# S5 states scanned in units of two pairs under the weight strips, with the unit's stores begun from ScalarE

## The reference

```
z = h @ w_in                                  # 1024 -> 5120 columns; u is 1024 of them
x_re = einsum('tbgc,gpc->tbgp', ug, bb_re)    # 64 groups of 16 channels, 64 complex states each
x_im = einsum('tbgc,gpc->tbgp', ug, bb_im)
h[t] = lam_bar * h[t-1] + x[t]                # diagonal, complex, the associative scan
y = einsum(h_re, c_re) - einsum(h_im, c_im) + d * u
y5 = gelu(y)
```

## Time and profile before

| quantity | value |
|---|---|
| median of 3 runs | 3718.71 us (3714.18 to 3720.71) |
| the profiled execution, its own time | 3713.49 us |
| its span, first to last instruction | 3711.7 us |
| PE busy | 3191.5 us, 86% |
| DVE busy | 1431.3 us, 39% |
| ACT busy | 1003.4 us, 27% |
| POOL busy | 936.7 us, 25% |
| TensorE clock granted, mean | 0.892 of full |
| DMA moved | 421.74 MB, 114 GB/s mean |

### The profile page before, as it was taken

One profiled execution on the slowest core, in us unless ns is written; L12 is line 12 of the kernel. 1 busy time (PEld: TensorE's weight loads), 2 busy tenths in 40 slices (PEclk: granted clock), 3 DMA queues, 4 the chain that ended last, 5 costly groups with the idle time before them and its releaser, 6 DMA issues. The chain is left out here.

```text
span 3711.7 us, 46938 instructions
## 1 busy us (share of the span) xinstructions
PE 3191.5 (86%) x16972; PEld 2891.6 (78%) x16972; DVE 1431.3 (39%) x2425; ACT 1003.4 (27%) x1675; POOL 936.7 (25%) x461
## 2 busy tenths in 40 slices
PE   7999985789938787499499978999999949999599
PEld 6999984678737676299488848999999948889487
DVE  6893396111961088443200022000000057776422
ACT  3211112211101143333200023111111168887122
POOL 2222340112501176011111200111111136554021
PEclk8999996999969999699799987999999966666799
DMA  4436332664325365442423222222222122323433
GB/s 129 127 122 206 117 98 61 167 179 137 108 70 157 113 239 162 165 119 85 170 90 110 82 79 88 68 68 68 68 77 76 51 100 89 113 85 99 158 136 109
DMA packets 374896, 421.74 MB, mean 114 GB/s; under 512 B 39937, under 2 KB 325249, under 8 KB 367665
## 3 DMA queue, kind: packets, MB, share of 16 engines
q1 hardware_dynamic: 204368, 315.69, 27.0%
q10 hardware_dynamic: 170464, 105.23, 9.1%
HBM read 273.66 MB, written 151.39 MB: 115 GB/s over the span
## 5 line engine op out<-in xcount | busy, mean ns | idle before, releaser
L1072 PE MATMUL p_psum<-p_h_hi,p_w_hi 128*128 128x344 f32 (+1 forms) x1600 | 566.4, 354 | 0.8 <-ACT p_y L777 0.8
L1072 PE MATMUL p_psum<-p_h_hi,p_w_lo 128*128 128x344 f32 (+1 forms) x1600 | 560.9, 351 | 0.0
L1072 PE MATMUL p_psum<-p_h_lo,p_w_hi 128*128 128x344 f32 (+1 forms) x1600 | 559.5, 350 | 0.0
L400 PE MATMUL p_psum<-p_h_hi,p_w_hi 128*128 128x408 f32 (+1 forms) x1280 | 448.5, 350 | 0.9 <-DVE p_h_lo L326 0.9
L400 PE MATMUL p_psum<-p_h_hi,p_w_lo 128*128 128x408 f32 (+1 forms) x1280 | 448.2, 350 | 0.0
L400 PE MATMUL p_psum<-p_h_lo,p_w_hi 128*128 128x408 f32 (+1 forms) x1280 | 448.0, 350 | 0.0
L1218 PE MATMUL c_psum<-c_wo_hi,c_m_hi 128*128 128x512 f32 (+1 forms) x816 | 319.2, 391 | 76.6 <-POOL c_m_lo L1202 76.6
L678 POOL CAST p_w_hi<-p_w_raw 128x1024 fp32r<-128x1024 f32 x80 | 105.5, 1319 | 936.5 <-PE p_psum L1072 772.8
L1072 PEld LDWEIGHTS p_psum<-p_h_hi,p_w_hi 128*128 128x128 f32 x1600 | 301.6, 189 | 34.0 <-issue 7.1
L1072 PEld LDWEIGHTS p_psum<-p_h_hi,p_w_lo 128*128 128x128 f32 x1600 | 301.6, 189 | 29.0
L1072 PEld LDWEIGHTS p_psum<-p_h_lo,p_w_hi 128*128 128x128 f32 x1600 | 301.7, 189 | 28.1
(11 more groups left out here) (276 smaller groups left out, 5599.8 us busy)
## 6 DMA issues: line engine op xcount, KB each, us to landing
p_w_raw<-in_w_in SPq DMA_DIRECT2D x112, 512.0 KB, 4.1
z<-p_out ACTq DMA_DIRECT2D x64, 512.0 KB, 3.2
z<-p_out ACTq DMA_DIRECT2D x32, 1024.0 KB, 5.6
hg_raw<-z SPq DMA_DIRECT2D x16, 2048.0 KB, 9.4
rt_raw<-z SPq DMA_DIRECT2D x16, 1536.0 KB, 7.0
p_u<-u_s SPq DMA_DIRECT2D x32, 584.0 KB, 7.9
c_m_raw<-m SPq DMA_DIRECT2D x16, 1024.0 KB, 6.7
u_s<-p_out SPq DMA_DIRECT2D x128, 73.0 KB, 3.3
```

What stands on the lines that cost most here:

```text
L400: ins = pe.matmul(psum[:, b, 0:n], w[par][:, k, :], h[:, k, c0:c0 + n], start=(k == 0 and j == 0), stop=(k == KD - 1 and j == 2))
L1072: ins = pe.matmul(bank, wv[par][:, k, :], h[:, k, c0:c0 + n], start=(k == 0 and j == 0), stop=(k == KD - 1 and j == 2))
```

## The change

The two jobs "into" and "out" and the scan over all pairs are replaced by one job, "unit", of two pairs (`UP = 2`, so `NU = 16` units a half), in strips 22 to 37 of the first half and 10 to 25 of the second. For each unit PE makes the contributions before the strip (`into`), DVE turns, scans and turns back the states of the two pairs while the strip runs (`unit`), and PE makes the outputs behind the strip (`out`). The scan is now the instruction `tensor_tensor_scan` with a real decay `mag8`; the complex turn is taken out by tables `turn_re` and `turn_im` of 32 x 129 elements each, which DVE makes once, ahead of the setup (`further`). The tile `x` is gone; the tables of the setup and the unit's tiles share one tile, `shared`. The loads of a unit (`load_unit`) are four: `wk`, `km`, `gs`, `u`. The gelu and the four stores of a unit are in ACT's list (`unit_stores`). Four loads fill `s_stack` at the start. The credit on `y_mm` is 2, and `y_mm` counts finished units.

```diff
-STRETCHES = (((0, 2, None), (2, 2, None), (4, 4, "setup"), (8, 12, "setup"), (20, 2, None), (22, 8, "into"),
-              (30, 8, None), (38, 2, None)),
-             ((0, 2, None), (2, 6, "out"), (8, 2, "out"), (10, 8, "into"), (18, 8, None), (26, 8, "out"),
-              (34, 4, None), (38, 2, None)))
+STRETCHES = (((0, 2, None), (2, 2, None), (4, 4, "setup"), (8, 12, "setup"), (20, 2, None), (22, 16, "unit"),
+              (38, 2, None)),
+             ((0, 2, None), (2, 6, None), (8, 2, None), (10, 16, "unit"), (26, 12, None), (38, 2, None)))
@@ SP
+            for c in range(2):
+                for q in range(2):
+                    sp.dma_start(s_stack[c * NP:(c + 1) * NP, :, q, :], a["s5_s0"][q * NP:(q + 1) * NP, c, :, :])\
+                        .then_inc(s5_ld, 16)
+            def load_unit(half, n, i, par):
+                sp.dma_start(wk[par], wt_dram[bass.ds(n * UP, UP)].rearrange("j p c n -> p j c n"))\
+                    .then_inc(slot_ld[par], 16)
...
-                            sp.wait_ge(x_mm, i * 8 + (32 * half + 4 * (q0 + par) + 4))
...
+                        if job == "unit":
+                            sp.wait_ge(y_mm, i * 2 + (NU * hf + par + 2))
+                            load_unit(hf, i * 2 + par, i, par)
...
+                    sp.wait_ge(k_done, NPAIR + 2)
+                    sp.wait_ge(kmat_st, 16 * L8)
@@ DVE, ahead of the setup's tables
+                dve.tensor_tensor(ta, turn_re[:, js, near], at_re, ALU.mult)
+                dve.tensor_tensor(tb, turn_im[:, js, near], at_im, ALU.mult)
+                dve.tensor_tensor(tc, turn_re[:, js, near], at_im, ALU.mult)
+                link(dve.tensor_tensor(td, turn_im[:, js, near], at_re, ALU.mult))
+                dve.tensor_tensor(turn_re[:, js, far], ta, tb, ALU.subtract)
+                link(dve.tensor_tensor(turn_im[:, js, far], tc, td, ALU.add))
+            k = 1
+            while k < CHH:
+                for part in range(max(1, k * NPAIR // D)):
+                    jn = min(NPAIR, D // k)
+                    further(k, part * jn, jn)
+                k *= 2
@@ DVE, a unit
+                step(dve.tensor_tensor(m_re[:, :, :, 1:XC], got[:, :, :, NS + 1:IN], re[:, :, :, 1:XC], ALU.mult))
+                step(dve.tensor_tensor(m_im[:, :, :, 1:XC], got[:, :, :, NS + 1:IN], im[:, :, :, 1:XC], ALU.mult))
...
+                        step(dve.tensor_tensor_scan(h_turned[:, jj, c, :], decay, h_in[:, jj, c, :], 0.0,
+                                                    ALU.mult, ALU.add))
@@ PE
-            pe.sem_inc(x_mm, 8)
-            pe.sem_inc(y_mm, 8)
+            pe.sem_inc(y_mm, 2)
...
+                pe.wait_ge(slot_ld[par], i * 64 + (64 * (NU // 2) * half + 64))
+                pe.wait_ge(hs_done, at + 1)
...
+                        if job == "unit":
+                            into(hf, i, par)
                         strip(hf, s0, i, par)
+                        if job == "unit":
+                            out(hf, i, par)
```

More of the change, by code:

```diff
@@ L545, in stores_before @@
             return CREDIT + sum(store_units(h, k) for h in range(2) for k in range(s % 2, N_P0, 2) if (h, k) < (hf, s))
[L547 to L554, removed]
         block = ctx.enter_context(nc.Block())
@@ L622, in two @@
                                     .then_inc(g_st[e], 16)
[L623 to L629, removed]
                 rounds(sp, n // 2, two)
@@ L653, in _ @@
             for s0, n, job in STRETCHES[1]:
[L654 to L658, removed]
+                if job == "unit":
                     for par in range(2):
                         sp.wait_ge(stored[par], stores_before(1, N_U + par))
-                if job == "out" and s0 > 20:
-                    sp.wait_ge(x_mm, 64 + 8)
                 strips(1, s0, n, job)
-            sp.wait_ge(scan_done, 3)
+            sp.wait_ge(hs_done, 2 * NU + 1)
             sp.dma_start(out_p, h_last[:]).then_inc(out_st, 16)
             sp.wait_ge(out_st, 32)
-            for pp in range(SLOT):
-                sp.wait_ge(y_st[pp], 32 * 2 * NSLOT + CREDIT)
+            for par in range(2):
+                sp.wait_ge(y_st[par], 64 * NU + CREDIT)
         @block.gpsimd
@@ L772, in two @@
[L772 to L778, removed]
@@ L779, in strips @@
-                rounds(act, n // 2, two)
+                        if job == "unit":
+                            act.wait_ge(y_mm, i * 2 + (NU * hf + par + 3))
+                            act.wait_ge(y_st[par], i * 64 + (64 * (NU // 2) * hf + CREDIT))
+                            for jj in range(UP):
+                                ins = act.activation(y[par][jj], ps[:, 6 + jj, 0:2 * YCH]
+                                                     .rearrange("p (q n) -> p q n", q=2), ACT.Gelu_apprx_tanh)
+                            ins.then_inc(y_done, 1)
+                            unit_stores(hf, i, par)
@@ new lines, in strips, with unit_stores @@
+                rounds(act, n // 2, two)
+            def unit_stores(half, i, par):
+                at = i * 2 + (NU * half + par)
+                act.wait_ge(y_done, at + 2)
+                for jj in range(UP):
+                    for c in range(2):
+                        row = (2 * UP * par + 2 * jj + c) * GC
+                        act.dma_start(y_dram[half, bass.ds(i * (4 * UP * GC) + row, GC), :, :]
+                                     .rearrange("o t c -> t o c"), y[par][jj][:, c, :]).then_inc(y_st[par], 16)
@@ L914, in _ @@
             dve.wait_ge(setup_done, 1)
+            dve.tensor_copy(cos8[:], cos[:])
+            dve.tensor_copy(sin8[:], sin[:])
+            link(dve.tensor_copy(mag8[:], mag[:]))
+            for _ in range(3):
+                dve.tensor_tensor(t0[:], cos8[:], cos8[:], ALU.mult)
+                dve.tensor_tensor(t1[:], sin8[:], sin8[:], ALU.mult)
+                dve.tensor_tensor(turns[:], cos8[:], sin8[:], ALU.mult)
+                link(dve.tensor_tensor(red[:], mag8[:], mag8[:], ALU.mult))
+                dve.tensor_tensor(cos8[:], t0[:], t1[:], ALU.subtract)
+                dve.tensor_scalar(sin8[:], turns[:], 2.0, None, ALU.mult)
+                link(dve.tensor_copy(mag8[:], red[:]))
@@ L916, in power_products @@
+            link(ins)
+            for c in range(2):
+                ins = dve.tensor_tensor(s_new[:, c], s_new[:, c], s_tmp[:, c], ALU.add)
+            ins.then_inc(setup_done, 1)
+            dve.wait_ge(setup_done, 2)
             def power_products(j, base, first, tmp, c):
@@ L1022, in stacks @@
-            def stacks(half):
-                with dve.Fori(0, NPAIR // 2) as i:
-                    for par in range(2):
-                        dve.wait_ge(y_mm, i * 2 + (NPAIR * half + par + 7))
-                        for q in range(2):
-                            for c in range(2):
-                                ins = dve.tensor_copy(h_stack[par][c * NP:(c + 1) * NP, q, :],
-                                                      x[q * NP:(q + 1) * NP, c, bass.ds(i * 2 + par, 1), NS:NS + YCH]
-                                                      .rearrange("p j n -> p (j n)"))
-                        ins.then_inc(hs_done, 1)
@@ new lines, in units @@
+            def units(half):
+                with dve.Fori(0, NU // 2) as i:
+                    for par in range(2):
+                        unit(half, i, par)
+            for e in range(2):
+                dve.wait_ge(wt_st[e], 16 * (NPAIR // 2) + CREDIT)
+                dve.wait_ge(g_st[e], 16 * (NPAIR // 2) + CREDIT)
+            dve.wait_ge(k_done, NPAIR + 2)
+            link(dve.memset(h_in[:, :, :, 0], 0.0))
+            dve.sem_inc(step_done, 1)
+            dve.sem_inc(hs_done, 1)
@@ L1074, in strip, with into, out @@
                     ins.then_inc(blk_done, 1)
+            def into(half, i, par):
+                at = i * 2 + (NU * half + par)
+                pe.wait_ge(slot_ld[par], i * 64 + (64 * (NU // 2) * half + 64))
+                pe.wait_ge(hs_done, at + 1)
+                for jj in range(UP):
+                    for q in range(2):
+                        for c in range(2):
+                            ins = pe.matmul(ps[q * NP:(q + 1) * NP, 4 + jj, c * IN:(c + 1) * IN],
+                                            wk[par][:, jj, c, q * NP:(q + 1) * NP],
+                                            u[par][:, 2 * jj + q, 0:IN], start=True, stop=True)
+                ins.then_inc(x_mm, 1)
+            def out(half, i, par):
+                at = i * 2 + (NU * half + par)
+                pe.wait_ge(hs_done, at + 2)
+                pe.wait_ge(y_done, at + 1)
+                for jj in range(UP):
+                    for q in range(2):
+                        bank = ps[:, 6 + jj, q * YCH:(q + 1) * YCH]
+                        pe.matmul(bank, km[par][:, 2 * jj + q, :], u[par][:, 2 * jj + q, UCH - YCH:UCH],
+                                  start=True, stop=False)
```

(9 more changed lines are left out.)

236 lines of the change are left out of this document (88 added, 148 removed).

## The result

| | median | runs | ratio to before |
|---|---|---|---|
| before | 3718.89 us | 3714.18 to 3720.71 | |
| after | 3862.31 us | 3858.87 to 3865.52 | 1.0388 (1.037 to 1.0406) |

A forecast was written before the change was run, and what follows sets the result against it. TensorE was taken as the bound wherever it has strips. Terms of +181 (first half), -33 (second half), +22, -43 and +2 gave +129 us on 3713.5, forecast as 3848 us against the runs' median, range 3785 to 3925 us.

The forecast's parts named there:

- a stop with its clock: TensorE between `out` and `into`: 6.5 us waiting for the load plus 2.7 us lost to a lower clock, 9.2 us.
- the setup: VectorE makes the turn tables ahead of the setup, 47 us of work, delaying TensorE: +22 us.
- first unit: First half's first load waits for the copies into `kmat`: 10 us plus 2.7 for the clock, +13 us.
- second prelude: Ahead of the second half, 6 us of waiting instead of 49, since VectorE is free: -43 us.
- first prelude: At the start, four loads of `s_stack` go ahead of the input tiles: +2 us, between 0 and 8.
- second half: TensorE's strips, units and stops in the second half: 632 us, before 665, so -33 us.
- The load has lost its lead: SyncE's count on `y_mm` puts each unit's whole load landing on TensorE's path; 30 stops cost 276 us.
- VectorE under a strip: A unit's turns and scans take VectorE 8.2 us, hidden by a strip of 11.2 us or more: costed at nothing.
- The stores from ScalarE: The y stores issued by ScalarE wait for nobody's next strip: costed at nothing.
- The short stop: Rival at the unit loads: a stop of 5.3 us and 1.7 for the clock, 3782 us; chance 0.13.
- the long one: Rival at the unit loads: stores share engines with the load, 9.0 + 3.0 us a stop, 3932 us; chance 0.14.
- hidden loads: Rival at the unit loads: the loads are hidden and the kernel is faster, 3572 us; chance 0.05.

The follow-up runs named there:

- x1: The change with SyncE's wait on `y_mm` one lower, so a unit's load may start one unit earlier: 3585.96 us, 0.9623 of before.
- x9: The change with 35 unread identity matmuls behind each `out` of the first half, filling the stop: 3848.82 us in one run.
- x8: x1 plus split load, turn tables for k = 32 and 64 behind the setup, only `km` waiting for `kmat`, `s_stack` loads behind input tiles: 3548.56 us, 0.9548 of before.
- x5: The change without y stores in the rounds, y written from two tiles at the stage's end: 3986.46 us in one run.
- x6: The change with 22 unread identity matmuls behind each `out` of the first half: 3854.98 us, 1.036 of before.

## Why the prediction was right

The sign, the mechanism and the size were right; the time was 14 us above the forecast and inside the range. By its steps:

| term | forecast | measured | from |
|---|---|---|---|
| a stop with its clock | 6.5 + 2.7 | 7.2 + 2.2 | rounds of the change against x1, x9 |
| 30 stops | 276 | 281 | (23.8 - 14.43) x 30 |
| the setup | +22 | +21.7 | start of strip 20: 327.3, before 301.05, less 4.5 |
| first unit | 10 + 2.7 | 10.4 and a slow strip | waits |
| second prelude | -43 | -43 | 29.0 against 72.0 |
| first prelude | +2 | +4.5 | strips begin at 45.6, before 41.1 |
| first half from strip 22 | +181 | +186 | windows |
| second half | -33 | -25 | windows |

**The load has lost its lead.** Shown by x1, where the count alone was altered. The two parts of a stop were off by 0.7 and 0.5 us in opposite ways. The row of an "into" load had 6.8 us from the first issue, and here it was 7.0 us in the mean with 0.2 us more ahead of it; I had taken 6.5 for both. The clock cost 2.2 us and not 2.7. That the 30 stops together came out within 5 us is in part luck: each error alone would have made 15 to 21. The Trainium skill, "DMA: Bandwidth & Descriptors", section "Anatomy of one DMA — SWDGE (gpsimd) path", states its sum for one transfer that GpSimd issues; worked out for these four as one it is an estimate of 4.5 us, and the wait was 7.2 us.

**The second half** was forecast 8 us too low. 15 stops at 9.4 and not 9.2 us make 3; 4 are in the spacing of a round without stops, 14.35 us in x1 where I had added 14.11 up from its parts, some 0.1 us at each of the three places where matmuls of one kind follow another. The last us is in the strips behind the prelude.

**The setup.** Shown by the timeline of VectorE in the change (a slow instruction beside GpSimd's split, one at its usual length, and the first `w_apart`):

```profile
96.52 3.30 DVE L908 TENSOR_TENSOR p_xt<-p_turn_re 128x1024 f32<-128x1024 f32 x1
...
113.19 1.22 DVE L912 TENSOR_TENSOR p_turn_re<-p_xt 128x1024 f32<-128x1024 f32 x1
...
120.25 0.36 DVE L958 COPY p_w_apart<-p_shared 64x32 f32<-64x32 f32 x2
```

The split of that strip (L663) ran on GpSimd from 95.49 us for 3.26 us. The first `w_apart` begins at 120.3, where I had 118; TensorE waited 15.7 us for it and 4.0 us in three later waits; the other 2 us of the term go with a lower clock there (0.95 on average until strip 20, before 0.99). That the forecast met it so closely is partly luck. Its printed steps don't give 22: the first `w_apart` at 118 against TensorE at 100.3 makes 18, and 47 less the 19.5 of slack makes 27.5. x8 shows that the term goes when a part of the tables moves behind the setup.

**The first prelude.** Four loads in pieces of 32 bytes ahead of the input tiles cost 4.5 us, between my bounds of 0 and 8; x8 had them behind the tiles and lost nothing. SyncE's timeline shows where: the four loads of the change, and the third and fourth input tile of the change, of before and of x8.

```profile
7.74 10.56 SPq L572 DMA_DIRECT2D p_s_stack<-in_s_s  x4
18.34 2.03 SPq L562 DMA_DIRECT2D p_xt<-in_x_prompt  x2
```

```profile
15.27 1.72 SPq L569 DMA_DIRECT2D p_xt<-in_x_prompt  x2
```

```profile
15.06 1.72 SPq L564 DMA_DIRECT2D p_xt<-in_x_prompt  x2
```

The tiles are issued 3.1 to 3.3 us later behind these loads; the rest of the 4.5 us is not traced.

**VectorE under a strip**: 7.4 us, costed at 8.2, hidden. **The stores from ScalarE**: hidden as forecast, and x5 shows that they don't slow the load either; what the prediction left out is how much their place is worth, 180 us and more, against SyncE's list.

**The rivals.** The short stop (7.0 us with its clock) and the long one (12.0) are both excluded by the rounds. The one on the other side, hidden loads, was priced at 3572 us; with the lead restored the kernel ran at 3586. Some 4 us of the difference between the spans of before and after lie behind the S5 stage (2428.7 against 2432.6 us from its last strip to the end), in stages that the change leaves alone. Over the profiles of the other kernels, x5 aside, that stretch lies between 2428.7 and 2435.4 us, so 4 us is no more than its scatter.

## What to carry to other kernels

Two buffers are not a lead: read from the wait's number which unit must be finished when a load is issued, and set against it what stands between that point and the load's user on the engine that waits. Then follow the issuing engine's own list, since a wait on the same unit's output ahead of the load undoes a correct count. A stop of a few us on TensorE costs its length and then some in the strip behind it; here 7.2 us cost 9.4.

## What the runs showed of the hardware

- Small products hold TensorE's clock when they fill the stop wholly: 128x128 identities, 0.23 us each, kept it at 1.00 (2.4 GHz) over fourteen rounds. With 5.07 us of them and 1.8 to 3.4 us of standing still behind (x6) it fell in most rounds and held in three.
- A `tensor_tensor_scan` of 129 elements took 0.345 us in a row of four, 1.38 us together, less than the 0.405 in the mean for 128 elements in the earlier trace rows.
- ScalarE loaded a table ahead of 16 evictions and of 16 gelus in this stage (1.28 us each), before ahead of three of each. TensorE has no wait for an eviction in this stage.
